# Decode keys of a paged attention turned by VectorE in 32x32 blocks inside SBUF, and scores as nine products of 32 rows

## The chip, the cores and the metric

The kernel runs on one core of a Trainium2 chip. The metric is the device time of one execution in microseconds (us); lower is better. The engines are TensorE (PE, its weight loads PEld), VectorE (DVE), ScalarE (ACT), GpSimd (POOL) and SyncE (SP). The last two also issue the transfers from the cache; SPq is SyncE's queue.

## What is computed

The reference is one decoder layer for a prompt of 1024 tokens and 8 decode sequences of 8 new tokens each: an RWKV-7 mixer, a latent attention (MLA), a pooling group, then a gated feed-forward net. The change touches the decode half of the attention. There, each of 8 sequences has 4096 old positions in pages of 128 rows (256 latent columns and 32 rope columns), found through a page table:

```python
ckv_past = cache_kv_latent[l][page_table].reshape(Bs, past_len, KV_RANK)
kr_past = cache_k_rope[l][page_table].reshape(Bs, past_len, B_ROPE_DIM)
q_lat = jnp.einsum('bthd,chd->bthc', q_nope, p['w_uk'])
s_past = (jnp.einsum('bqhc,blc->bhql', q_lat, ckv_past) + jnp.einsum('bqhr,blr->bhql', q_rope, kr_past)) * scale
s_new = (jnp.einsum('bqhc,bkc->bhqk', q_lat, ckv) + jnp.einsum('bqhr,bkr->bhqk', q_rope, kr)) * scale
s_new = jnp.where(pos[None, :] <= pos[:, None], s_new, -jnp.inf)
pr = jax.nn.softmax(jnp.concatenate([s_past, s_new], axis=-1), axis=-1)
o_lat = jnp.einsum('bhql,blc->bqhc', pr[..., :L], ckv_past) + jnp.einsum('bhqk,bkc->bqhc', pr[..., L:], ckv)
```

## The kernel before

The kernel is a sequence of stages with a barrier between them (`new_stage`, line 154). Everything here is float32. Three stages matter, and each engine's work is a list written out by hand, in order, with semaphores between the engines.

*Latent stage* (lines 641 to 834). It norms and rotates the latent rows, writes them out, and keeps three copies of the 64 new ones: by rows (`ckv_new`, line 767), latent turned (`ckvT_new`, 761) and rope turned (`krT_new`, 725 and 739).

*Queries stage* (1183 to 1255). TensorE turns `w_uk` (1212), VectorE copies it (1240), TensorE makes the latent queries of six heads (1218), and VectorE and ScalarE spread them into `q_lat` (1232). `q_rope` holds four versions of the rope queries, each on its own 32 rows with zeros elsewhere (1227).

*Decode stage* (1258 to 1571). Eight sequences are four pairs x; the two of a pair (f = 0, 1) take the two halves of 64 output rows, 6 heads x 8 tokens in each. The 32 pages of a sequence are 8 groups of four, so a pair has 8 key steps and a ninth with the new keys: 36 steps s, 32 of them with a load j. A load is, for each of the two sequences, four pages of 128 KB into a slot (128 partitions x 4 rows x 256) and their rope rows. There are five pairs of slots (NL), and loads 0 and 1 (EARLY) are issued a stage earlier. SyncE issues the transfers of f = 0 and one rope page of f = 1 (`load_rows`, 872, 875 and, the ninth, 879), GpSimd the other seven of f = 1. Each reads its page number from SBUF first. Both wait for a free slot, that is for the values of the load five before (`all_loads`, 1289).

A key step does this:

- `turn_keys` (1306): TensorE turns a slot's keys by transposes of 128x128 into three PSUM banks, eight latent (1319) and one rope (1320), once for each f. VectorE copies half (1431) and ScalarE the rest (1530, 1531) into SBUF. They wait for the copies of the half before.
- `dscores` (1322): rope products (1335), then latent products (1339), 128 rows deep, two column halves side by side, into one of two banks.
- `softmax_max` (1440): VectorE's maximum (1448) and bias (1450). Then ScalarE's exps (1539).
- `turn_weights` (1351): TensorE turns the 128x512 weights (1357), VectorE copies them (1438).
- `dvalues` (1362): weights times the rows of the slot (1375), two halves of it on either side of the turned weights; VectorE copies the part (1458).
- The nine parts of a pair are joined on VectorE (1487) while the next pair runs, then turned (1389).

TensorE's order in step s is: scores(s), keys of the next step f = 0, first half of values(s-1), keys f = 1, turned weights(s), second half of values(s-1):

```python
dscores(s)
if following:
    turn_keys(following[0] * NG + following[1], 0)
if s >= 1:
    dvalues(s - 1, 0)
if following:
    turn_keys(following[0] * NG + following[1], 1)
turn_weights(s)
if s >= 1:
    dvalues(s - 1, 1)
```

## Time and profile before

| | us |
|---|---|
| median of 3 runs | 2031.93 (2031.01 to 2033.15) |
| the profiled execution | 2032.99 |
| its span | 2031.3 |
| TensorE busy, share | 1872.9, 92% |
| VectorE busy | 979.4, 48% |
| ScalarE busy | 514.9, 25% |
| GpSimd busy | 255.5, 13% |
| queries stage | about 458 to 465 |
| decode stage | about 465 to 732 |

A line of a timeline gives the start, the duration, the engine, the line of the kernel, the operation, what it writes and reads, the tile (rows * columns of the array), the moving shape, and how many instructions are merged in it; in brackets the engine's idle time before and what ended it. A float32 product on TensorE stands as two records, each of two passes over its columns; a transpose stands as one. Ends of TensorE's records are modelled and include a tail of 0.2 to 0.3 us, in which the next ones already run. PEclk is the granted clock: 1.00 is 2.4 GHz, 0.50 is 1.2 GHz.

### The profile page before, as it was taken

Reading aid. Unit: us, or ns where it says so; the run is one execution under the profiler, and the core shown is the slowest. Engines: PE = TensorE matmul, PEld = TensorE weight load, DVE = VectorE, ACT = ScalarE, POOL = GpSimd, SP = SyncE. Lnnn points to the kernel's source line nnn. Section 1 sums busy time; section 2 is a strip of 40 time slices with the busy share of each in tenths; the row PEclk is TensorE's granted clock in tenths of the full one; section 3 lists DMA queues with packets and bytes.
Section 4 is the critical chain, followed back from the end, with each engine's and each line's share of the span. In section 5 each row is a group of like instructions: output and inputs, shape, how many; then the busy total and the mean of one; then the engine's idle time right before and its main releaser. Section 6 shows DMA issues by size and latency. Waiting matters only on the chain. (4 is left out here: it accounts for less than half of the span.)

```text
span 2031.3 us, 39649 instructions
## 1 busy us (share of the span) xinstructions
PE 1872.9 (92%) x16034; PEld 1642.3 (81%) x16034; DVE 979.4 (48%) x1800; ACT 514.9 (25%) x1064; POOL 255.5 (13%) x440
## 2 busy tenths in 40 slices
PE   5999998998999965999898979999999999999997
PEld 5999984665666632888746979999999999999996
DVE  6232426674455557544245335545545535445455
ACT  5111123542223333222124321111111111111113
POOL 1000004324444312000001210000000000000000
PEclk8999999998999965999867989999999999999999
DMA  7111113104555400000032111021021021110203
GB/s 231 53 42 53 40 43 83 33 8 129 155 156 155 119 25 0 4 4 4 18 120 64 32 32 42 22 73 37 27 63 42 27 67 32 42 53 24 64 20 110
DMA packets 148258, 119.19 MB, mean 59 GB/s; under 512 B 22900, under 2 KB 136298, under 8 KB 147805
## 3 DMA queue, kind: packets, MB, share of 16 engines
q1 hardware_dynamic: 138189, 97.35, 16.3%
q0 software_dynamic: 9744, 18.78, 3.4%
q8 instruction: 128, 2.10, 0.4%
q10 hardware_dynamic: 144, 0.52, 0.1%
q14 instruction: 53, 0.43, 0.1%
HBM read 102.81 MB, written 11.44 MB: 56 GB/s over the span
## 5 line engine op out<-in xcount | busy, mean ns | idle before, releaser
L202 PE MATMUL bank<-normed2T_hi,w_hi 128*128 128x384 f32 (+1 forms) x1056 | 346.0, 328 | 4.3 <-DVE w_lo L492 4.3
L203 PE MATMUL bank<-normed2T_hi,w_lo 128*128 128x384 f32 (+1 forms) x1056 | 345.7, 327 | 0.0
L204 PE MATMUL bank<-normed2T_lo,w_hi 128*128 128x384 f32 (+1 forms) x1056 | 345.7, 327 | 0.0
L202 PEld LDWEIGHTS bank<-normed2T_hi,w_hi 128*128 128x128 f32 x1056 | 199.1, 189 | 5.5 <-DVE w_lo L492 5.5
L203 PEld LDWEIGHTS bank<-normed2T_hi,w_lo 128*128 128x128 f32 x1056 | 199.1, 189 | 0.0
L204 PEld LDWEIGHTS bank<-normed2T_lo,w_hi 128*128 128x128 f32 x1056 | 199.0, 188 | 0.0
L202 PE MATMUL bank<-inner_hi,w_hi 128*128 128x384 f32 (+1 forms) x528 | 174.5, 330 | 10.2 <-DVE w_lo L492 7.1
L492 DVE TENSOR_TENSOR w_lo<-work,w_hi 128x1024 fp32r<-128x1024 f32 (+2 forms) x120 | 118.6, 989 | 131.1 <-ACT w_hi L487 129.9
L204 PE MATMUL bank<-inner_lo,w_hi 128*128 128x384 f32 (+1 forms) x528 | 174.0, 330 | 0.0
L203 PE MATMUL bank<-inner_hi,w_lo 128*128 128x384 f32 (+1 forms) x528 | 173.7, 329 | 0.0
L202 PE MATMUL bank<-normedT_hi,w_hi 128*128 128x384 f32 (+3 forms) x480 | 157.6, 328 | 5.6 <-DVE w_lo L492 5.6
L203 PE MATMUL bank<-normedT_hi,w_lo 128*128 128x384 f32 (+3 forms) x480 | 157.3, 328 | 0.0
L204 PE MATMUL bank<-normedT_lo,w_hi 128*128 128x384 f32 (+3 forms) x480 | 157.3, 328 | 0.0
L487 ACT CAST w_hi<-work 128x1024 fp32r<-128x1024 f32 (+2 forms) x120 | 102.3, 858 | 214.6 <-PE bank L204 209.0
L2742 DVE TENSOR_TENSOR residualT<-bank,residualT 128x384 f32<-128x384 f32 x144 | 76.1, 534 | 128.0 <-PE bank L204 127.8
L202 PEld LDWEIGHTS bank<-inner_hi,w_hi 128*128 128x128 f32 x528 | 99.6, 189 | 11.7 <-DVE w_lo L492 8.4
L2687 DVE TENSOR_TENSOR work<-bank,rwkv_streamsT 128x384 f32<-128x384 f32 (+1 forms) x66 | 33.9, 514 | 154.4 <-PE bank L204 152.2
L2658 ACT ACTIVATE rwkv_streamsT<-rwkv_streamsT 128x1088 f32<-128x1088 f32 x22 | 24.5, 1114 | 313.7 <-DVE rwkv_streamsT L2708 313.7
L203 PEld LDWEIGHTS bank<-inner_hi,w_lo 128*128 128x128 f32 x528 | 99.7, 189 | 0.0
L204 PEld LDWEIGHTS bank<-inner_lo,w_hi 128*128 128x128 f32 x528 | 99.6, 189 | 0.0
L2648 POOL COPY rwkv_streamsT<-work 128x2 f32<-128x2 f32 x22 | 4.1, 186 | 727.9 <-DVE work L2691 727.9
L202 PEld LDWEIGHTS bank<-normedT_hi,w_hi 128*128 128x128 f32 (+1 forms) x480 | 90.0, 188 | 5.9 <-DVE w_lo L492 5.7
(411 smaller groups left out, 3353.0 us busy)
## 6 DMA issues: line engine op xcount, KB each, us to landing
work<-in_w_up_dram SPq DMA_DIRECT2D x44, 512.0 KB, 3.9
residualT<-in_cache_kv_latent_dram SPq DMA_DIRECT2D x80, 128.0 KB, 2.4
residualT<-in_cache_kv_latent_dram POOLq DMA_DIRECT2D x80, 128.0 KB, 2.6
work<-in_w_in_dram SPq DMA_DIRECT2D x19, 512.0 KB, 3.8
work<-in_w_down_dram SPq DMA_DIRECT2D x32, 256.0 KB, 2.8
weight_ring<-in_cache_kv_latent_dram POOLq DMA_DIRECT2D x48, 128.0 KB, 2.6
weight_ring<-in_cache_kv_latent_dram SPq DMA_DIRECT2D x48, 128.0 KB, 2.4
residualT<-residual_spill SPq DMA_DIRECT2D x1, 4352.0 KB, 15.4
```

Source lines behind the costliest of these rows:

```text
L202: pe.matmul(out, w[0], x[0], start=first, stop=False)
L203: pe.matmul(out, w[1], x[0], start=False, stop=False)
L204: return pe.matmul(out, w[0], x[1], start=False, stop=last)
L487: act.copy(wsp[i % 2][0][:, 0:m[0], 0:m[1]], raw[:, 0:m[0], 0:m[1]]).then_inc(done, 1)
L492: dve.tensor_tensor(wsp[i % 2][1][:, 0:m[0], 0:m[1]], raw[:, 0:m[0], 0:m[1]], wsp[i % 2][0][:, 0:m[0], 0:m[1]].bitcast(F32), ALU.subtract) ...
L2648: nc.gpsimd.tensor_copy(gend[:, 0:2, f], p_seq[:, SEQ - 2:SEQ])
L2658: nc.scalar.activation(hraw, cv, ACT.Tanh, scale=0.5).then_inc(f_tanh, 1)
L2687: ins = dve.tensor_tensor(p_seq[:, t0:t0 + k], PS[g % 8][:, 0:k], rstd[:, t0:t0 + k], ALU.mult)
L2742: dve.tensor_tensor(xT[:, m, t0:t0 + n], PS[(3 * j + c) % 8][:, 0:n], xT[:, m, t0:t0 + n], ALU.add).then_inc(f_dn, 1)
```

## The change

The keys are no longer turned by TensorE. VectorE transposes each slot in blocks of 32x32 (`dve.transpose`), SBUF to SBUF, into `key_t`. In a block the columns (latent or rope) then lie on 32 partitions, and the four groups of 32 partitions hold different keys. So a score is a sum of nine products of 32 rows (eight latent, one rope), made for each of four row groups q (into PSUM banks 0 to 3) and two column halves f: 72 products of 128 columns a step. Two steps take turns in the columns of the same banks. The queries are laid out to match (`q_blk`: each block of 32 on all four groups); for that the `w_uk` blocks are spread four times ahead of the product. VectorE turns two loads before the first step, and load j + 2 after the maximum of step j. The copies of the turned weights and of the parts move from VectorE to ScalarE. The values are one piece now, ahead of the turned weights, and TensorE's order is scores(s), values(s-1), turned weights(s). The new keys are turned by VectorE in the queries stage from 288 columns. The joined result has its own place (`o_t`). The loads, their order and their waits are as before. The core of the diff:

```diff
-        PS = [ctx.enter_context(nc.psum_tensor(f"bank{i}", [P, 512], F32)) for i in range(8)]
+        banks8 = ctx.enter_context(nc.psum_tensor("bank", [P, 8 * 512], F32))
+        PS = [banks8[:, 512 * i:512 * (i + 1)] for i in range(8)]
...
+        KB = RANK // 32 + 1
+        cw = Carve(WORK - KB * QN)
+        q_blk = cw.take(KB * QN).rearrange("p (b x f c) -> p b x f c", b=KB, x=NX, f=2)
+        w_uk_b = wring[:, 0:3 * 4 * RANK].rearrange("p (m b q c) -> p m b q c", m=3, b=KB - 1, q=4)
+        o_t = spare[:, 0:2 * QN].rearrange("p (k q) -> p k q", k=2)
...
+            def rope_queries(eng_copy, groups):
+                for h in range(H):
+                    r0 = ROPE * (h % 4)
+                    for g in groups:
+                        dst = q_blk[ROPE * g:ROPE * (g + 1), KB - 1, :, :, h * TS:(h + 1) * TS]
+                        eng_copy(dst.rearrange("p x f c -> p f x c"), of_sample(rp[r0:r0 + ROPE, h // 4, SEQ:T]))
+            def latent_queries(eng_copy, h):
+                src = PS[h].rearrange("p (b f x t) -> p b f x t", b=KB - 1, f=2, x=NX)
+                for f in range(2):
+                    eng_copy(q_blk[:, 0:KB - 1, :, f, h * TS:(h + 1) * TS], src[:, :, f])
+            def spread_w(eng_copy, m):
+                src = PS[7 - m][:, 0:RANK].rearrange("p (b c) -> p b c", b=KB - 1)
+                return eng_copy(w_uk_b[:, m], src.unsqueeze(2).broadcast_to([P, KB - 1, 4, 32]))
             @block.gpsimd
             def _(pool):
-                nc.gpsimd.memset(q_rope[:, 2:4], 0.0).then_inc(s_q0, 1)
-                nc.gpsimd.memset(q_lat, 0.0).then_inc(s_q0, 1)
+                nc.gpsimd.memset(q_blk[:, :, :, :, H * TS:HD], 0.0).then_inc(s_q0, 1)
+                pool.wait_ge(s_q0, 1)
+                rope_queries(nc.gpsimd.tensor_copy, (2, 3))
...
-                for h in range(H):
-                    eng_copy(by_half(q_lat[:, k], h),
-                             of_sample(PS[4 + k + 2 * (h % 2)][:, (h // 2) * NS:(h // 2 + 1) * NS]))
+                        pe.transpose(PS[7 - m][:, k * P:(k + 1) * P],
+                                     w_uk[:, k, m * P:(m + 1) * P], ident).then_inc(wu_t, 1)
+                for m in range(3):
+                    pe.wait_ge(wu_cp, m + 1)
+                    for b in range(KB - 1):
+                        for f in range(2):
+                            r = slice(HD * f, HD * f + HD)
+                            last = pe.matmul(PS[2 * m + f][:, b * NS:(b + 1) * NS],
+                                             w_uk_b[r, m, b].rearrange("p q c -> p (q c)"), qn[r, m, SEQ:T],
+                                             start=True, stop=True)
+                    last.then_inc(ql_mm, 1)
...
-                dve.memset(q_rope[:, 0:2], 0.0).then_inc(s_qr, 1)
-                dve.wait_ge(wu_t, 1)
                 for m in range(3):
-                    dve.tensor_copy(w_ukT[:, m], PS[m][:, 0:RANK]).then_inc(wu_cp, 1)
-                dve.wait_ge(s_qr, 1)
-                rope_queries(dve.tensor_copy, (0, 1))
-                dve.wait_ge(ql_mm, 1)
-                dve.wait_ge(s_q0, 2)
-                latent_queries(dve.tensor_copy, 0)
+                    dve.wait_ge(wu_t, 2 * m + 2)
+                    spread_w(dve.tensor_copy, m).then_inc(wu_cp, 1)
+                dve.transpose(new_t, ckv_new).then_inc(s_nt, 1)
+                for m in range(3):
+                    dve.wait_ge(ql_mm, m + 1)
+                    latent_queries(dve.tensor_copy, 2 * m)
             @block.scalar
             def _(act):
-                act.wait_ge(s_q0, 1)
-                rope_queries(nc.scalar.copy, (2, 3))
-                act.wait_ge(ql_mm, 1)
-                act.wait_ge(s_q0, 2)
-                latent_queries(nc.scalar.copy, 1)
+                rope_queries(nc.scalar.copy, (0, 1))
+                for m in range(3):
+                    act.wait_ge(ql_mm, m + 1)
+                    latent_queries(nc.scalar.copy, 2 * m + 1)
...
-        keyT = cw.take(2 * 2 * 2 * 512).rearrange("p (s f k c) -> p s f k c", s=2, f=2, k=2)
-        krT = cw.take(2 * 2 * P).rearrange("p (s f c) -> p s f c", s=2, f=2)
-        pr = cw.take(2 * 512).rearrange("p (s c) -> p s c", s=2)
-        prT = cw.take(2 * 4 * P).rearrange("p (s c) -> p s c", s=2)
+        KT = 4 * RANK + P
+        key_t = cw.take(2 * 2 * KT).rearrange("p (s f c) -> p s f c", s=2, f=2)
+        pr = spare[:, 2 * QN:2 * QN + 2 * 512].rearrange("p (s c) -> p s c", s=2)
+        prT = spare[:, 2 * QN + 2 * 512:2 * QN + 4 * 512].rearrange("p (s c) -> p s c", s=2)
...
-                def turn_keys(j, f):
-                    slot = 2 * (j % NL) + f
-                    pe.wait_ge(s_k[f][j % NL], (128, 112)[f] * (j // NL + 1))
-                    if f == 1:
-                        pe.wait_ge(s_kx[j % NL], 16 * (j // NL + 1))
-                    n = 2 * j + f
-                    if n >= 1:
-                        pe.wait_ge(k_cpa, n)
-                        pe.wait_ge(k_cpb, 2 * n)
-                    rows = kslot[slot].rearrange("p (r c) -> p r c", r=4)
-                    for k in range(2):
-                        for r in range(4):
-                            pe.transpose(PS[k][:, r * P:(r + 1) * P], rows[:, r, k * P:(k + 1) * P], ident)
-                    pe.transpose(PS[2][:, 0:P], krr[:, slot, :], ident).then_inc(k_t, 1)
                 def dscores(s):
                     x, g = steps[s]
-                    bank = PS[3 + s % 2]
                     if s >= 2:
                         pe.wait_ge(dp_exp, s - 1)
-                    q = [(slice(HD * f, HD * f + HD), slice(x * P + HD * f, x * P + HD * f + HD)) for f in range(2)]
                     if g < NG:
                         j = x * NG + g
-                        pe.wait_ge(k_cpa, 2 * j + 2)
-                        pe.wait_ge(k_cpb, 4 * j + 4)
-                        for r in range(4):
-                            for f, (out, cols) in enumerate(q):
-                                pe.matmul(bank[out, r * P:(r + 1) * P], q_rope[:, r, cols], krT[:, j % 2, f, :],
-                                          start=(r == 0), stop=False, skip_group_check=True)
-                        for k in range(2):
-                            for f, (out, cols) in enumerate(q):
-                                last = pe.matmul(bank[out, :], q_lat[:, k, cols], keyT[:, j % 2, f, k, :],
-                                                 start=False, stop=(k == 1), skip_group_check=True)
-                    else:
-                        for k in range(2):
-                            for out, cols in q:
-                                pe.matmul(bank[out, 0:NS], q_lat[:, k, cols], ckvT_new[:, k], start=(k == 0),
-                                          stop=False, skip_group_check=True)
-                        for out, cols in q:
-                            last = pe.matmul(bank[out, 0:NS], q_rope[:, 2, cols], krT_new, start=False, stop=True,
-                                             skip_group_check=True)
+                        pe.wait_ge(k_t, 2 * j + 2)
+                    for b in range(KB):
+                        for q in range(4 if g < NG else 2):
+                            rows = slice(32 * q, 32 * q + 32)
+                            for f in range(2):
+                                out = PS[q][HD * f:HD * f + HD, P * (s % 2):P * (s % 2) + P]
+                                if g < NG and b < KB - 1:
+                                    keys = key_t[rows, j % 2, f, 0:4 * RANK].rearrange("p (r c) -> p r c", r=4)
+                                    keys = keys[:, :, 32 * b:32 * b + 32]
+                                    out = out.rearrange("p (r c) -> p r c", r=4)
+                                elif g < NG:
+                                    keys = key_t[rows, j % 2, f, 4 * RANK:KT]
+                                else:
+                                    keys, out = new_t[rows, 32 * b:32 * b + 32], out[:, 0:32]
+                                last = pe.matmul(out, q_blk[rows, b, x, f, :], keys, start=(b == 0),
+                                                 stop=(b == KB - 1), skip_group_check=True)
                     last.then_inc(ds_mm, 1)
...
-                def dvalues(s, part_of):
+                def dvalues(s):
...
-                pe.wait_ge(s_nm, 16)
-                turn_keys(0, 0)
-                turn_keys(0, 1)
...
-                    following = s + 1 < NSTEP and steps[s + 1][1] < NG and steps[s + 1]
                     dscores(s)
                     if g == JOINED and x >= 1:
                         turn_joined(x - 1)
-                        pe.wait_ge(j_cp, x)
-                    if following:
-                        turn_keys(following[0] * NG + following[1], 0)
                     if s >= 1:
-                        dvalues(s - 1, 0)
-                    if following:
-                        turn_keys(following[0] * NG + following[1], 1)
+                        dvalues(s - 1)
                     turn_weights(s)
-                    if s >= 1:
-                        dvalues(s - 1, 1)
-                for half in range(2):
-                    dvalues(NSTEP - 1, half)
+                dvalues(NSTEP - 1)
...
             def _(dve):
-                def copy_keys(j, f):
-                    dve.wait_ge(k_t, 2 * j + f + 1)
+                def turn_keys(j):
                     if j >= 2:
                         dve.wait_ge(ds_mm, step_of(j - 2) + 1)
-                    dve.tensor_copy(keyT[:, j % 2, f, 0, :], PS[0][:, :]).then_inc(k_cpa, 1)
-                def copy_weights(s):
-                    dve.wait_ge(dp_t, s + 1)
-                    if s >= 2:
-                        dve.wait_ge(do_mm, s - 1)
-                    n, w = (P, 4 * P) if steps[s][1] < NG else (NS, P)
-                    dve.tensor_copy(prT[0:n, s % 2, 0:w], PS[5][0:n, 0:w]).then_inc(dp_cp, 1)
+                    for f in range(2):
+                        slot = 2 * (j % NL) + f
+                        dve.wait_ge(s_k[f][j % NL], (128, 112)[f] * (j // NL + 1))
+                        if f == 1:
+                            dve.wait_ge(s_kx[j % NL], 16 * (j // NL + 1))
+                        dve.transpose(key_t[:, j % 2, f, 0:4 * RANK], kslot[slot])
+                        dve.transpose(key_t[:, j % 2, f, 4 * RANK:KT], krr[:, slot, :]).then_inc(k_t, 1)
...
-                        dve.tensor_tensor(bank[:, 0:NS], bank[:, 0:NS], newmask[:, x], ALU.add).then_inc(ds_mask, 1)
+                        dve.tensor_tensor(src, src, newmask[:, x].rearrange("p (q c) -> p q c", q=2), ALU.add
+                                          ).then_inc(ds_mask, 1)
                         dve.wait_ge(ds_mask, x + 1)
-                    dve.tensor_reduce(mx[:, x, g:g + 1], bank[:, 0:w], AX_X, ALU.max).then_inc(ds_max, 1)
+                    dve.tensor_reduce(mx[:, x, g:g + 1], src, AX_XY, ALU.max).then_inc(ds_max, 1)
...
-                copy_keys(0, 0)
-                copy_keys(0, 1)
+                dve.wait_ge(s_nm, 16)
+                turn_keys(0)
+                turn_keys(1)
                 for s in range(NSTEP):
                     x, g = steps[s]
-                    following = s + 1 < NSTEP and steps[s + 1][1] < NG and steps[s + 1]
                     softmax_max(s)
-                    for half in range(2):
-                        if following:
-                            copy_keys(following[0] * NG + following[1], half)
-                    copy_weights(s)
-                    if s >= 1:
-                        copy_part(s - 1)
+                    if g < NG and x * NG + g + 2 < len(loads):
+                        turn_keys(x * NG + g + 2)
...
+                    if g < NG:
+                        dst = pr[:, s % 2, :].rearrange("p (r q c) -> p q r c", r=4, q=4)
+                        src = banks8[:, 0:4 * 512].rearrange("p (q w) -> p q w", q=4)
+                        src = src[:, :, P * (s % 2):P * (s % 2) + P].rearrange("p q (r c) -> p q r c", r=4)
+                    else:
+                        dst, src = pr[:, s % 2, 0:NS].rearrange("p (q c) -> p q c", q=2), scores_of(s)
+                    nc.scalar.activation(dst, src, ACT.Exp, bias=bias[:, x, g:g + 1], scale=SCALE,
                                          accum_out=sums[:, x, g:g + 1]).then_inc(dp_exp, 1)
+                def copy_weights(s):
+                    act.wait_ge(dp_t, s + 1)
+                    if s >= 2:
+                        act.wait_ge(do_mm, s - 1)
+                    n, w = (P, 4 * P) if steps[s][1] < NG else (NS, P)
+                    nc.scalar.copy(prT[0:n, s % 2, 0:w], PS[4][0:n, 0:w]).then_inc(dp_cp, 1)
+                def copy_part(s):
+                    x, g = steps[s]
+                    act.wait_ge(do_mm, s + 1)
+                    if g == 0 and x >= 2:
+                        act.wait_ge(j_ready, x - 1)
+                    nc.scalar.copy(part[:, x % 2, g, :], PS[6 + s % 2][:, 0:RANK]).then_inc(do_cp, 1)
...
-                    following = s + 1 < NSTEP and steps[s + 1][1] < NG and steps[s + 1]
+                    exps(s)
                     if g == JOINED and x >= 1:
                         copy_joined(x - 1)
-                    if following:
-                        copy_keys(following[0] * NG + following[1], 0)
-                    exps(s)
-                    if following:
-                        copy_keys(following[0] * NG + following[1], 1)
+                    if s >= 1:
+                        copy_part(s - 1)
+                    copy_weights(s)
                     if g == 1 and x >= 1:
                         join_weights(x - 1)
+                copy_part(NSTEP - 1)
```

## Rows read from the trace of the kernel before

**Rows 1.** Busy time by stretch: start:end, length, PE, PEld, DVE, ACT, POOL, PEclk, DMA share, GB/s.
```profile
476.50:719.00 242.50, 235.21 (x1999) 152.68 (x1997) 120.46 (x252) 72.07 (x203) 97.90 (x198) 1.00 0.49 141
744.00:760.00 16.00, 12.49 (x29) 6.47 (x28) 9.30 (x8) 8.94 (x11) 4.89 (x2) 0.50 0.00 0
```

**Rows 2.** Timeline of TensorE over one key step.
```profile
567.79 1.09 PE L1319 MATMUL bank<-constants,weight_ring 128*128 128x128 f32 x8
...
568.92 1.08 PE L1375 MATMUL bank<-residualT,work 128*64 128x256 f32 x8
...
571.08 0.60 PE L1357 MATMUL bank<-constants,work 128*128 128x128 f32 x4
...
572.52 1.04 PE L1335 MATMUL bank<-work 128*64 128x128 f32 x16
573.39 1.89 PE L1339 MATMUL bank<-work 128*64 128x512 f32 x8
575.21 0.33 PE L1319 MATMUL bank<-constants,weight_ring 128*128 128x128 f32 x1
```

**Rows 3.** Timeline of SyncE's queue in the decode stage: load 2, its ninth, the last.
```profile
466.02 0.33 SPq L872 DMA_DIRECT2D residualT<-in_cache_kv_latent_dram  x1
...
473.15 0.32 SPq L879 DMA_DIRECT2D residualT<-in_cache_k_rope_dram  x1
474.24 0.32 SPq L872 DMA_DIRECT2D weight_ring<-in_cache_kv_latent_dram  x1
...
701.27 0.32 SPq L879 DMA_DIRECT2D residualT<-in_cache_k_rope_dram  x1
```

**Rows 4.** Transfers of the decode stage: KB each, median us to landing.
```profile
residualT<-in_cache_k_rope_dram SPq DMA_DIRECT2D x150, 16.0 KB, 2.3
```

**Rows 5.** Timeline of GpSimd: first and last large transfer of load 4.
```profile
478.87 0.49 POOL L872 DMA_DIRECT2D weight_ring<-in_cache_kv_latent_dram  x1 [0.65 <-issue]
...
484.01 0.49 POOL L872 DMA_DIRECT2D weight_ring<-in_cache_kv_latent_dram  x1 [0.64 <-issue]
```

**Rows 6.** Timelines of VectorE and ScalarE in the same step.
```profile
567.91 0.69 DVE L1448 TENSOR_REDUCE work<-bank 128x1 f32<-128x512 f32 x1 [1.25 <-PE bank L1339]
568.63 0.15 DVE L1450 TENSOR_SCALAR work<-work 128x1 f32<-128x1 f32 x1
...
573.08 0.99 DVE L1487 SCALAR_TENSOR_TENSOR work<-work 128x256 f32<-128x256 f32 x2
...
569.67 0.70 ACT L1539 ACTIVATE work<-bank,work 128x512 f32<-128x512 f32 x1
570.25 0.21 ACT L1539 ACTIVATION_READ_ACCUMULATOR work<-bank,work 128x1 f32 x1
```

**Rows 7.** Timelines of TensorE with small tiles, outside the decode stage.
```profile
811.14 0.94 PE L1892 MATMUL bank<-work,rwkv_streamsT 64*64 64x128 f32 x24
811.91 0.52 PE L1901 MATMUL bank<-rwkv_streamsT,work 64*64 64x64 f32 x24
...
748.75 1.65 PE L1685 MATMUL bank<-weight_ring 32*128 32x384 f32 x4
```

**Rows 8.** Groups of VectorE's instructions: busy us, mean ns, idle before.
```profile
L2719 DVE TENSOR_TENSOR rwkv_streamsT<-rwkv_streamsT 128x1088 f32<-128x1088 f32 x22 | 28.4, 1292 | 0.8
L1713 DVE TENSOR_TENSOR_SCAN work<-work 128x1152 f32<-128x1152 f32 x3 | 7.7, 2557 | 7.8 <-ACT work L1632 7.8
```

**Rows 9.** Timelines of TensorE and VectorE in the queries stage.
```profile
458.18 0.85 PE L1212 MATMUL bank<-constants,residualT 128*128 128x128 f32 x6 [1.55 <-PEq L158]
460.32 2.88 PE L1218 MATMUL bank<-work,weight_ring 64*128 64x64 f32 x24 [1.30 <-DVE weight_ring L1240]
...
463.24 0.88 DVE L1232 COPY work<-bank 128x64 f32<-128x64 f32 x6 [0.71 <-PE bank L1218]
```

**Rows 10.** The stage's end: VectorE's mask of step 35, the next stage's first transfer.
```profile
718.38 0.23 DVE L1446 TENSOR_TENSOR bank<-bank,residualT 128x64 f32<-128x64 f32 x1
...
732.81 0.37 SPq L1607 DMA_DIRECT2D weight_ring<-in_c_heads_dram  x1
```

101 lines of the change are left out of this document (29 added, 72 removed).

## Prediction, made before the changed kernel was seen

> **What bounds the kernel now.** I read four views in this order: the stretches of the decode stage, the timeline of TensorE over one step, the timeline of SyncE's queue, and that of GpSimd's. The stretches say that TensorE is busy 235.2 of 242.5 us at the full clock (1.00, 2.4 GHz), while VectorE is busy half of it [rows 1]. So the stage looks bound by TensorE. Its step takes 575.21 - 567.79 = 7.42 us (a quiet one 7.33): two turns of keys (each 8 + 1 transposes, about 1.1 us), two halves of the values (1.08 us each), the turned weights (0.60), the rope part of the scores (1.04) and the latent part (1.89) [rows 2].
>
> The third view changes that. SyncE issues nine transfers for each of the loads 2 to 31. After the ninth of a load (L879) the first of the next follows 1.09 to 1.10 us later in 28 of 29 cases (1.59 in the other, behind a slow issue); [rows 3] show the first of them. That is the time SyncE takes to read a page number and issue, so the wait for a free slot never holds it: SyncE is saturated from its first issue at 466.02 to its last at 701.27. The ninths are (701.27 - 473.15) / 29 = 7.87 us apart on average, 7.39 at best. **SyncE's pace is a bound of 7.87 us a load, level with TensorE's 7.33**; TensorE starts with two loads in hand and reaches the last load some 5 us after it has landed. GpSimd needs 484.01 - 478.87 = 5.14 us for a load's first to last large transfer and about 1.15 to the next load, 6.3 in all [rows 5], so it has 1.6 us of slack. The change touches no transfer. Whatever it takes off TensorE, the stage can't end before the last load has landed, 701.27 + 2.3 = 703.6 [rows 3, 4], plus the chain behind it.
>
> **The change, part by part.** *Removed per key step on TensorE:* 18 transposes (about 2.1 us) and the old scores (1.04 + 1.89, together 2.7 without overlap) [rows 2], and four copies of keys on VectorE and ScalarE (VectorE's at about 0.69 us, what its maximum over as many elements out of PSUM takes [rows 6]).
>
> *Added on TensorE:* 9 blocks x 4 row groups x 2 column halves = 72 products of 128 columns. A float32 product stands as two records, so 144. One record of 512 columns takes 1.89 / 8 = 0.24 us with two halves side by side, that is 0.43 alone (2 x 512 / 2.4 GHz); one of 128 columns then takes 0.107 alone. How many run side by side? 24 records of 128 columns on four tiles of 64x64 took 0.94 us with a tail of 0.27, so 29 ns each or a little less, near 107 / 4 [rows 7]. L1685 works on groups of 32 rows: two products of 384 columns took 1.65 us at 1.2 GHz, where one record is 0.64, so four in a row would be 2.6: neighbouring 32-row groups do overlap. Eight tiles give 144 x 107 / 8 = 1.92 us, plus tail 2.2; if only four overlap, 144 x 26.7 = 3.84, plus tail 4.1. I take 2.2, since nothing in the rows shows a limit at four.
>
> A rule that speaks against the change was weighed here. 24 records of 64 columns took 0.52 us with a tail of 0.22, 13 ns each [rows 7]. The Trainium skill (TensorEngine Tiling (Array Packing), Instruction Overhead) says that each matmul costs some 60 cycles however short it is, 25 ns at 2.4 GHz; by it the 144 records would be an estimated 3.6 us and the sum 2 to 3 us longer at its end. The row disagrees, and I go by the row.
>
> *Added on VectorE:* per load two turns of 128x1024 and two of 128x128, straight from the slots. No row shows this instruction. Two-input work in SBUF takes 1292 ns for 1088 elements, 1.19 ns each; a scan takes 2557 for 1152, 2.2 each [rows 8]. So 1.22 + 0.29 = 1.5 us a half and 3.0 a load, or at the scan's rate 2.7 and 5.4; I take the first, as moving is nearer to a plain pass than to a recurrence. A lower end (a fast plain mode) would be half. With the maximum (0.69 + 0.15) and joins (0.99) a step costs VectorE 4 to 5 us [rows 6], 7.2 at the scan's rate: under 7.87 either way. The weights' and parts' copies move to ScalarE, which has exps (0.70 + 0.21) and little else now: 0.9 + 0.7 + 0.5 = 2 us.
>
> *The new chain of a step.* From the end of scores(s): maximum and bias 0.95, exps 0.9, with two hops 2.05; meanwhile values(s-1) take 1.7 to 1.8; weights turned 0.5; scores(s+1) 2.2. Together 4.8 us, again below 7.87. VectorE now turns load j+2 between the maxima of steps j and j+1 and so waits in line for the transfer; maximum j+1 is queued behind it, and TensorE, which needs exps for its next turned weights, waits too. **The stage becomes bound by SyncE's issues alone**, with TensorE busy about 4.6 us of 7.87.
>
> *The end of the stage.* The last ninth lands at 703.6; its half is turned by 705.2; maximum 30 by 706.2; exps 707.1; weights turned 707.8; scores(31) 710.0; step 35, the last with new keys, has its scores at 710.0 + 2.05 + 0.5 + 1.2 = 713.8. Before, that point was 718.38 and the next stage's first transfer came 14.4 us later, at 732.81 [rows 10]. Behind it the new order puts one ScalarE copy ahead of the join's weights and takes one copy off VectorE: 14.9. So 728.7, **-4.1 us**, at the full clock. With TensorE idle three microseconds in every eight the clock may fall: 16 us with TensorE busy 78% ran at 0.50 [rows 1]. At 1.2 GHz scores, values and turned weights cost 4.1, 3.6 and 0.9 us and the chain is 8.4 to 9, so TensorE would fall behind, be dense, and get its clock back. The end is then 734 to 736, +1 to +3. I take the middle: -1.
>
> *The stage of the queries, ahead of it.* All of SyncE's issues wait behind it, so each microsecond here is a microsecond at the end. Before: 458.2 to 464.1 [rows 9]. After: three spread copies that write 1024 elements each (1.13 us apart, from 458.8, the first done at 460.0, the last at 462.3), the new rows' turn 0.45, then 3 x 16 products of 64 rows by 128 columns, 96 records of 64 columns where 24 took 2.88 us (0.11 each beyond the tail, clock falling to 0.5). There four records in a row used the same row group; now the group changes every two. As two groups overlap in [rows 7], 57 ns a record, 1.8 us for each of three parts: 461.9, 463.7, 465.5, then two VectorE copies, 466.7. That is +2.6. If they don't overlap: 3.5 us each, done at 471.5, +7.4. If the clock stays up, the spread copies bind: +1.3. Rope copies (12 on ScalarE, 12 on GpSimd at about 0.24) end by 463 and hide below this; uncovered they'd cost nothing, as the products end later. The latent stage loses a small GpSimd memset and copy and a VectorE copy that lay in waits, and its last copy grows by 32 columns: 0.
>
> **Sum.** -1 + 2.6 = +1.6 us on a span of 2031.3. The profiled execution took 2032.99, 1.06 above the median 2031.93, so I forecast 2034.6 for it and **2033.5 for the median**.
>
> **The rivals.** (a) *Slower by the queries' stage* (chance 0.22): products of alternate row groups don't overlap, +7.4, and TensorE's low clock at the end, +2: about 2041. For it: 0.11 us a record in [rows 9]. Against: L1685 and L1892. It decides once the stage lasts over 5 us more than before.
> (b) *Slower since TensorE's row groups or VectorE's turns bind* (0.08): with only two tiles side by side, scores take 144 x 53 ns = 7.7, the step 10.3, and 32 x (10.3 - 7.4) = +93: 2125. The same sign comes from GpSimd being held up while VectorE turns keys: 6.3 + 3.0 = 9.3 a load, +46. Against: GpSimd's 1.6 us of slack must be used up first. The Trainium skill (SBUF — State Buffer, Who interferes with whom) says that only the port pair shared by VectorE and GpSimd contends, as an exclusive lock; no row here shows whether a turn takes it.
> (c) *Faster* (0.20): SyncE's slow issues (0.47 us a load above its best of 7.39) become rarer with less going on beside them, and the clock stays up: up to -13.6, say 2023. For it: they come singly and at no fixed place. Against: the same transfers still run.
> (d) *Nothing to be seen* (0.50): my forecast, within 4 us either way. That the change does what it says is not in doubt from its text; it only doesn't touch the bound.
>
> **Range.** From 2023 (fast issues in part, full clock, +1.3) to 2044 (a queries' stage +7.4, low clock +3, turns at the scan's rate +2). Left out: (b) and half of (c). Counting 0.2% (4 us) as what a measurement can tell from no change: faster 0.20, same 0.50, slower 0.30.
>
> **What would show it.** L879's records: still 7.9 us apart, L872 following by 1.10. No wait of SyncE. TensorE busy 60 to 80% in the stage, with gaps of 2 to 3 us before the turned weights. VectorE idle until transfers land. Scores of about 2.2 us at clock 1.00; turns of about 1.2 us. The decode stage starting near 467.4. Wrong would be: L879 further apart than 8.3 (GpSimd or a slot holds it), scores over 4 us, turns over 2.4, or the queries' stage over 9 us.

## The result and the profile after

The changed kernel takes 2047.25 us at the median of 4 runs (2044.93 to 2054.67), the kernel before 2031.47 beside it (2029.04 to 2033.15): ratio 1.0081, interval 1.0066 to 1.0097. It is slower by 16 us, where 1.6 were forecast; the range ended at 2044. A second series of both gave 2047.84 and 2030.74, ratio 1.0090 (1.0075 to 1.0104). The profiled execution has a span of 2053.0 us, 21.7 more than before, and is the longest of the first four runs.

First the queue that bounds the stage. This is the timeline of SyncE's queue in the changed kernel (start, duration, engine, line): the stage's first transfer, load 2, the last ninth transfer (L873, before L879), and the first transfer of the stage behind.

```profile
472.56 0.42 SPq L1301 DMA_DIRECT2D residualT<-in_w_uv_dram  x1
473.78 0.33 SPq L866 DMA_DIRECT2D residualT<-in_cache_kv_latent_dram  x1
...
719.71 0.59 SPq L873 DMA_DIRECT2D residualT<-in_cache_k_rope_dram  x1
749.58 0.37 SPq L1572 DMA_DIRECT2D weight_ring<-in_c_heads_dram  x1
```

Beside [rows 3] and [rows 10] these four lines hold the loss. Load 2 starts at 473.78 where it started at 466.02: +7.8. Of this 0.7 lies ahead of the queries' stage, whose first transpose on TensorE starts at 458.84 where it started at 458.18 [rows 9], so the stage itself takes 7.1 us more. From load 2 to the last ninth it takes 245.9 us where it took 235.3: +10.7. From the last ninth to the next stage it takes 29.9 us where it took 31.5: -1.7. Together +16.8 at the stage's border. The rest of the kernel took 1303.4 us in this execution and 1298.5 before, +4.9; in the second profile of the changed kernel it took 1297.6, so nothing lasting stands behind that. That second profile, of a faster execution (span 2041.7), has the same three marks of SyncE's queue at

```profile
469.39 0.33 SPq L866 DMA_DIRECT2D residualT<-in_cache_kv_latent_dram  x1
716.24 0.32 SPq L873 DMA_DIRECT2D residualT<-in_cache_k_rope_dram  x1
744.15 0.37 SPq L1572 DMA_DIRECT2D weight_ring<-in_c_heads_dram  x1
```

that is +3.4, +11.6 and -3.6 beside the kernel before. The middle term is the one that stays.

The stretches of the changed kernel (columns as in [rows 1]): the products of the queries' stage, the decode stage, and its end.

```profile
460.50:471.00 10.50, 10.43 (x96) 10.32 (x96) 4.16 (x8) 2.59 (x10) 2.28 (x10) 0.50 0.01 2
479.00:720.00 241.00, 175.72 (x5118) 128.39 (x5113) 118.13 (x226) 53.92 (x138) 100.75 (x204) 0.88 0.53 147
744.00:760.00 16.00, 6.35 (x44) 2.64 (x44) 4.96 (x13) 8.11 (x9) 0.00 (x0) 0.50 0.25 77
```

TensorE is relieved: 175.7 busy us of 241, 73%, where it had 235.2 of 242.5. But its records rose from 1999 to 5118. The timelines of TensorE and of VectorE over one step of the changed kernel:

```profile
567.19 3.18 PE L1357 MATMUL bank<-residualT,mixedT 128*64 128x256 f32 x16
570.30 0.66 PE L1340 MATMUL bank<-constants,mixedT 128*128 128x128 f32 x4
570.89 2.32 PE L1330 MATMUL bank<-work 32*64 32x128 f32 x144
...
571.46 1.25 DVE L1406 STREAM_TRANSPOSE work<-weight_ring 128x1024 f32<-128x1024 f32 x1 [2.80 <-DMA residualT<-in_cache_k_rope_dram]
572.63 0.27 DVE L1407 STREAM_TRANSPOSE work<-residualT 128x128 f32<-128x128 f32 x1
```

The scores take 2.32 us, a turn 1.25 and 0.27. And VectorE's waits in the stage, longest first (total us, times, longest), name what the stage waits for: the ninth transfer of a load.

```profile
DVE work L1406 <- DMA residualT<-in_cache_k_rope_dram: 101.7, 35, 6.1
DVE work L1417 <- PE bank L1330: 12.6, 7, 3.1
```

So the stage did become bound by the arrival of the loads. What failed is the forecast that they would keep their pace. The ninths are (719.71 - 480.97) / 29 = 8.23 us apart, not 7.87, and still the next load's first transfer follows at 1.08 to 1.10 us in 28 of 29 cases: SyncE isn't waiting, it is issuing more slowly. Of the stage's 270 issues, 50 last over 0.36 us where 27 did, and the time beyond 0.32 us adds up to 21.6 us where it was 10.7. That difference, 10.9, accounts for the +10.7 of the stretch. The second profile agrees: again 8.23 us from ninth to ninth, 46 slow issues with 22.1 us.

What goes with them is in the view of the DMA queues, one queue's line (packets, MB, share), first of the kernel before over 464 to 703 us, then of the changed one over 472 to 722 us:

```profile
q8 instruction: 16, 0.26, 0.5%
```

```profile
q8 instruction: 41, 0.67, 1.2%
```

q8 fetches instructions, in packets of 16 KB. The slow issues lie at a fixed place behind them: 38 of the 41 fetches after, and 13 of the 16 before, have a slow issue that ends 1.2 to 1.9 us behind the fetch's start, with a median of 1.4 and 1.5. Fetches at random times would have met some 6 and 1. The slow issues that lie so hold 19.3 us of excess after and 7.7 before; all the others hold 2.3 after and 3.0 before. So the whole increase belongs to issues behind a fetch, and each fetch costs about the same in either kernel, 0.47 and 0.48 us. One of them, in the changed kernel (queue q8 over 566.5 to 567.0 us, and SyncE's queue):

```profile
q8 instruction: 1, 0.02, 14.6%
```

```profile
566.38 0.32 SPq L866 DMA_DIRECT2D weight_ring<-in_cache_kv_latent_dram  x1
566.89 1.23 SPq L869 DMA_DIRECT2D residualT<-in_cache_k_rope_dram  x1
```

The number of fetches fits the code. TensorE has 2 x 5118 instructions in the stretch, a weight load with each record; 41 packets make 250 for each. Before it was 2 x 1999 and 16, again 250. The Trainium skill (Runtime: NRT & Kernel Launch, Instruction fetch mechanics) says that fetches come in blocks of 16 KiB, 256 instructions; the rows agree. It also says that they are hidden behind the pace of the instructions. Whether that holds for the engine that fetches was not looked at; here another engine's queue shows them, 10.9 us / 25 = 0.44 us for each more.

### The profile page after: what moved, and what is told of

It reads as the page before. It is cut to its first block and busy times, and to the rows that moved or that the text cites. A ratio compares the mean times of both kernels' runs of the same rounds, so it can differ in the third digit from the quotient of the medians.

```text
span 2053.0 us, 46577 instructions
## 1 busy us (share of the span) xinstructions
PE 1825.5 (89%) x19610; PEld 1631.7 (79%) x19610; DVE 987.2 (48%) x1779; ACT 500.8 (24%) x1008; POOL 257.0 (13%) x449
## 5 line engine op out<-in xcount | busy, mean ns | idle before, releaser
L1330 PE MATMUL bank<-work 32*64 32x128 f32 x4608 | 92.0, 306 | 20.3 <-issue 15.8
L1330 PEld LDWEIGHTS bank<-work 32*64 32x64 f32 x4608 | 80.6, 148 | 29.8 <-issue 24.7
```

Of the source, the lines that this page charges most:

```text
L1330: last = pe.matmul(out, q_blk[rows, b, x, f, :], keys, start=(b == 0), stop=(b == KB - 1), skip_group_check=True)
```

## Experiments

The experiments set one theory against its rivals. **Theory I:** SyncE's issuing bounds the changed kernel's stage; with it goes theory F, that it was slowed by the fetches for TensorE's larger number of instructions. **The rivals:** something behind it binds as well (TensorE at a low clock, VectorE, GpSimd), or the slowing comes from VectorE's turns. The queries' stage was a question of its own.

### Does SyncE's issuing bound? One of nine issues moved, in either kernel

The ninth transfer goes to ScalarE, behind its copy of the parts:

```diff
-            if f == 0:
+            if f == 0 and ninth:
...
-                    load_rows(eng, j, f)
+                    load_rows(eng, j, f, ninth=False)
...
                     if s >= 1:
                         copy_part(s - 1)
+                        x0, g0 = steps[s - 1]
+                        if g0 < NG and x0 * NG + g0 + NL < len(loads):
+                            ninth(x0 * NG + g0 + NL)
```

> The changed kernel with the ninth transfer of each load (the rope rows of group 1's fourth page) issued by ScalarE after its copy of the parts, not by SyncE: SyncE issues 8 transfers a load instead of 9, nothing else moves. In the changed kernel the distance from one ninth to the next is 8.23 us on average over 29, and SyncE goes from the ninth to the next load's first in 1.10 us in 28 of 29, so it never waits. Theory I (SyncE's issuing bounds the stage): one of nine issues and its page load gone, the pace drops to 7.1 to 7.4 us a load, the stage is 24 to 33 us shorter and the kernel 2015 to 2024 us. Rival V (TensorE, VectorE or the DMA queues of GpSimd bind just behind): pace 7.8 to 8.2, kernel within 12 us of the changed one.

Measured: 2018.16 us (2011.21 to 2023.16), 0.9949 of the kernel before (0.9926 to 0.9972), 29 us below the changed kernel (27 by the two ratios). From load 2's first issue to load 31's the pace is (675.80 - 465.65) / 29 = 7.25 us a load, 8.23 in the changed kernel. This is theory I, inside both its ranges: one issue in nine, with its page load, is worth 1.0 us a load. The whole +0.36 a load of the change is smaller than that.

> The same move made in the kernel before: the ninth transfer issued by ScalarE at the end of a key step. Before, SyncE's pace is 7.87 us a load, and TensorE is busy 235.2 of 242.5 us of the stage, so its own need is 7.35 us a load or less. Theory I: SyncE no longer binds, TensorE does, at 7.35 to 7.6 us a load; kernel 6 to 14 us faster than before. Rival T (TensorE already is the bound there, and SyncE's pace follows it): 0 to 2 us. Both say that the move gains more in the changed kernel than here, by 12 us or more under I.

Measured: 2030.71 us, 1.0006 of the kernel before (0.9995 to 1.0017). Rival T was right here: theory I's 6 to 14 us did not come. The stretch of the decode stage, and SyncE's waits in it:

```profile
476.50:719.00 242.50, 234.96 (x1993) 152.20 (x1991) 119.66 (x249) 72.06 (x203) 98.00 (x199) 1.00 0.49 140
```

```profile
SPq L864 <- PE bank L1375: 29.4, 18, 5.6
```

Now SyncE waits 29.4 us for free slots, which come free by TensorE's values (L1375), and TensorE is busy 235 of 242.5 us exactly as in [rows 1]. So before the change TensorE bound the stage, and SyncE, which never waited either, ran at nearly the same pace beside it. A queue that never waits is not by that the only bound; taking an issue from it told the two apart.

### What slows SyncE's issues? Fewer and more instructions on TensorE, no turns on VectorE

Fewer: the scores of the key steps are summed over 5 of the 9 blocks; the first four are left out.

```diff
-                    for b in range(KB):
+                    for b in (range(4, KB) if g < NG else range(KB)):
...
```

> The changed kernel with only 5 of the 9 blocks of 32 rows in the scores of the key steps (the first four blocks of the latent rows left out of the sum). One look, for SyncE's pace in the decode stage. Theory F (what slowed SyncE from 7.87 to 8.23 us a load are TensorE's instructions: the stage's instruction fetches rose from 16 to 41 with TensorE's records from 1999 to 5118, and SyncE's issues longer than 0.36 us from 27 to 50, their excess over 0.32 us from 10.7 to 21.6 us, 0.44 us for each more fetch): 2048 records fewer, 25 fetches, excess 14 to 15 us, pace 7.99 us a load. Rival D (VectorE's turns of 32x32, or the clock, slow SyncE): the excess stays 20 us or more and the pace 8.15 or more.

Measured: 2036.67 us (a single run), pace (709.23 - 479.44) / 29 = 7.92 us a load, 30 slow issues, 12.1 us of excess. The queue of instructions over 472 to 712 us:

```profile
q8 instruction: 26, 0.43, 0.8%
```

That is theory F's 25 fetches, with the same turns on VectorE and the same transfers; the slowing shrank somewhat more than expected (7.99 and 14 to 15 were forecast).

No turns: the latent rows are turned for the first two loads only; the later scores use those old keys.

```diff
-                        dve.transpose(key_t[:, j % 2, f, 0:4 * RANK], kslot[slot])
+                        if j < 2:
+                            dve.transpose(key_t[:, j % 2, f, 0:4 * RANK], kslot[slot])
```

> The changed kernel with the turns of the latent rows by VectorE left out after the first two loads (scores are then of old keys; the rope rows are still turned). One look. Theory F: SyncE's excess and pace stay as they are, 20 us or more and 8.15 to 8.3 us a load, though VectorE is 78 us less busy. Rival D (VectorE's turns hold up SyncE or the transfers): excess near 11 us, pace near 7.87.

Measured: 2047.9 us (a single run), pace 8.13, 45 slow issues with 18.1 us of excess. The stretch of the stage, and the queue of instructions over 474 to 720 us:

```profile
481.00:717.00 236.00, 174.49 (x5103) 126.51 (x5108) 54.65 (x166) 53.92 (x138) 99.87 (x202) 0.88 0.52 149
```

```profile
q8 instruction: 42, 0.69, 1.1%
```

VectorE is busy 54.7 us in place of 118 and the pace hardly moves; the excess is 3 us less, below what F allowed (20) and far from D's 11. The excess scatters by as much without any such edit: in the five profiles that issue nine transfers a load on SyncE with the turns and the products of the scores in place it is 18.7 to 23.0 us, at paces of 8.16 to 8.30. VectorE's turns are not the cause. Nor is the clock: it is 0.88 here as in the changed kernel, and 0.86 with five blocks, where the loads came faster.

More: each product of the key steps' scores in two halves. The instructions are all there, but their sums are no longer the scores (why was not settled), so it is read for its time alone.

```diff
...
+                                    for c in range(2):
+                                        last = pe.matmul(out[:, :, w * c:w * c + w], q_blk[rows, b, x, f, :],
+                                                         keys[:, :, w * c:w * c + w], start=(b == 0),
+                                                         stop=(b == KB - 1), skip_group_check=True)
```

> The changed kernel with each product of the key steps' scores cut in two halves of 64 columns (144 products a step in place of 72, same work). One look. Theory F: 4608 records more in the stage, 77 fetches, SyncE's excess 37 us, pace 8.77 us a load, the stage some 15 us longer. Rival D: excess and pace as in the changed kernel, 21.6 us and 8.17 to 8.26. TensorE itself has room: its scores take 2.3 to 3.5 us of 8.2 a load, twice that would be 7.0 at the most beside 2.9 for the rest, so at the low clock it could bind; then SyncE's gap between loads would rise over 1.10 us.

Measured: 2135.25 us (a single run), where theory F expected some 15 us over the changed kernel. The stretch, the longest wait of VectorE, and the queue of instructions over 472 to 787 us:

```profile
480.00:785.00 305.00, 249.58 (x8927) 190.90 (x8925) 113.32 (x219) 52.44 (x131) 99.95 (x202) 0.80 0.40 117
```

```profile
DVE work L1426 <- PE bank L1335: 187.8, 29, 8.0
```

```profile
q8 instruction: 72, 1.18, 1.6%
```

VectorE waits 188 us for the scores, none of its long waits is for a transfer any more, and SyncE waits for slots (gaps of up to 8.4 us): TensorE binds, at (784.23 - 479.48) / 29 = 10.5 us a load. The fetches came (72 for 77), SyncE's excess rose to 29.8 us (37 expected), but with a queue that waits a slow issue costs nothing, so the pace tests neither theory. One thing it does show: halving the streamed columns did not halve a product's price. The next section finds the same of other products.

| kernel | fetches in the stage | slow issues, excess us | of it behind a fetch | us a load |
|---|---|---|---|---|
| before | 16 | 27, 10.7 | 7.7 | 7.87 |
| five blocks | 26 | 30, 12.1 | 9.9 | 7.92 |
| changed | 41 | 50, 21.6 | 19.3 | 8.23 |
| no turns | 42 | 45, 18.1 | 16.9 | 8.13 |
| two halves | 72 | 51, 29.8 | 29.5 | 10.5 (TensorE) |

The column "of it behind a fetch" counts the excess of slow issues that end 1.2 to 1.9 us behind a fetch's start. It is 0.38 to 0.48 us for each fetch in all five kernels; the differences between neighbouring rows are no finer than the scatter just named.

These runs change the number of TensorE's instructions and its fetches together; that it is the fetches, and not TensorE's activity, rests on where the slow issues lie. Why a fetch holds up an issue on another engine was not settled.

### What do the products of the queries' stage cost?

The products of 64 rows by 128 columns cut in two halves of 64 weight columns (the first kernel), or in two halves of 32 streamed columns with all 128 weight columns loaded for each (the second). The diff is the first kernel's:

```diff
-                            last = pe.matmul(PS[2 * m + f][:, b * NS:(b + 1) * NS],
-                                             w_uk_b[r, m, b].rearrange("p q c -> p (q c)"), qn[r, m, SEQ:T],
+                            for c in range(2):
+                                last = pe.matmul(PS[2 * m + f][64 * c:64 * c + 64, b * NS:(b + 1) * NS],
+                                                 w_uk_b[r, m, b, 2 * c:2 * c + 2].rearrange("p q c -> p (q c)"),
+                                                 qn[r, m, SEQ:T], start=True, stop=True)
```

> The changed kernel with the products of the queries' stage cut in two halves of 64 weight columns each (192 records of 64*64 in place of 96 of 64*128; same work). In the changed kernel the 96 records take 10.51 us, 107 to 109 ns each, at a granted clock of 0.50 throughout. Theory W (a record costs its 128 weight columns, one after another, and 64*64 tiles go beside each other as the 24 records of 64*64 of the output projection do in 0.52 and 0.94 us, 22 to 39 ns each): 192 records take 4.2 to 7.5 us, the decode stage's first transfer comes 3 to 6 us earlier, the kernel is 3 to 6 us faster than the changed one. Rival S (products of 64 rows don't go beside each other in any tiling; a record costs its columns in full, 53 ns at half the size): 192 records take 10.2 us or more, no gain.

> The changed kernel with each product of the queries' stage cut in two halves of 32 streamed columns instead, with the same 128 weight columns loaded for each (192 records). One look, for the stage's products alone. If the loading of 128 weight columns sets the 107 ns, the 192 records take 20.5 us (107 ns each). If loading and streaming add up (64 and 64 columns' worth), 15 to 16 us. If only streaming counts (the two row groups not overlapping), 10.5 us or less (53 ns each).

> The changed kernel itself, on the same chip as the next run, to see what the earlier 5.4 us of the decode stage's start are worth in the kernel's time. 1.0075 to 1.0085 of the kernel before, 2046 to 2049 us.

> The changed kernel with the queries' products in 64*64 tiles again. Its profiled run showed the 192 products in 4.7 us, the decode stage's first transfer at 468.41 in place of 473.78 us and the next stage's first at 744.12 in place of 749.58, but its median was only 1.6 us below the changed kernel's, with runs 12 us apart. If the 5.4 us hold to the end, 4.5 to 6 us faster than the changed kernel beside it. If the low granted clock comes later or elsewhere and takes them back: 0 to 3 us.

The timeline of TensorE in that stage, of the changed kernel in its first and in its second profile, of the weight halves (second series), and of the streamed halves (2050.09 us, a single run):

```profile
460.57 10.51 PE L1231 MATMUL bank<-work,weight_ring 64*128 64x64 f32 x96 [0.88 <-DVE weight_ring L1212]
```

```profile
461.11 5.58 PE L1231 MATMUL bank<-work,weight_ring 64*128 64x64 f32 x96 [0.88 <-DVE weight_ring L1212]
```

```profile
459.19 2.82 PE L1232 MATMUL bank<-work,weight_ring 64*64 64x64 f32 x146 [0.88 <-DVE weight_ring L1212]
462.50 0.92 PE L1232 MATMUL bank<-work,weight_ring 64*64 64x64 f32 x46 [0.49 <-issue]
```

```profile
459.19 18.23 PE L1232 MATMUL bank<-work,weight_ring 64*128 64x32 f32 x192 [0.88 <-DVE weight_ring L1212]
```

The clock over these products in the first profile stands in the stretch shown above (0.50); in the second it is 1.00:

```profile
461.10:466.70 5.60, 5.58 (x96) 5.44 (x96) 3.99 (x7) 2.53 (x10) 2.22 (x10) 1.00 0.01 3
```

And over 463 to 467 us of the kernel with the streamed halves:

```profile
463.00:467.00 4.00, 4.00 (x41) 4.00 (x40) 0.76 (x2) 0.65 (x2) 0.00 (x0) 0.50 0.00 0
```

Three things follow. The same 96 records cost 109 ns each at 1.2 GHz and 58 ns at 2.4 GHz. Halving the streamed columns with the weight columns kept leaves a record at 98 ns at 1.2 GHz (4.00 us for 41), where 107 was expected of the loading alone, 80 if loading and streaming added up, and 53 of the streaming alone. So **the price is, nearly all of it, the loading of 128 weight columns, one record after another**, though they lie in 64 rows and take turns between two row groups. The Trainium skill (TensorE: Matmul & The Clock Gate, LDWEIGHTS (loading the stationary operand)) gives the time as columns divided by 1.2, independent of the rows, 107 ns; the row at 1.2 GHz agrees, the one at 2.4 GHz shows half of it. And in 64*64 tiles a record costs 19 ns, 146 in 2.82 us: tiles of this size do go beside each other, theory W.

What this is worth is read from the stage's own length, from its first transpose on TensorE to load 2, since the stage doesn't start at the same time in every execution (455.6 to 459.4 over the twelve profiles of the changed kernel and its variants). The first transposes of the changed kernel in its two profiles and of the weight halves in the second series:

```profile
458.84 0.84 PE L1224 MATMUL bank<-constants,residualT 128*128 128x128 f32 x6 [1.56 <-PEq L159]
459.38 0.85 PE L1224 MATMUL bank<-constants,residualT 128*128 128x128 f32 x6 [1.55 <-PEq L159]
457.46 0.85 PE L1224 MATMUL bank<-constants,residualT 128*128 128x128 f32 x6 [1.55 <-PEq L159]
```

Load 2 follows at 473.78, 469.39 and 466.14. So the stage takes 14.9 us at the low clock and 10.0 at the full one, where the kernel before took 7.8 (466.02 - 458.18), and 8.7 with the weight halves (9.2 in their first profile, from 459.23 to 468.41). In both profiles of the halves the clock over the products was 1.00. The change costs the stage +7.1 at the low clock and +2.2 at the full one, and the halves leave +0.8 to +1.3 of it.

In the kernel's time the halves gave 2045.66 us (2040.29 to 2052.55) in the first series, 1.0085 of the kernel before (1.0055 to 1.0116) beside the changed kernel's 1.0081: no gain to be seen. In the second series they gave 2044.63 beside 2047.84, 1.0068 (1.0056 to 1.0080) beside 1.0090 (1.0075 to 1.0104): 3 to 4.5 us, with intervals that overlap a little, and less than the 4.5 to 6 expected. A gain of that size fits a stage that is 0.8 to 1.3 us shorter in executions with the full clock and 5.8 to 6.3 in those with the low one, (if the halves keep the full clock, as in their two profiles), but the kernel's time alone doesn't show it. Which executions the low clock meets wasn't settled: the six profiles with this unchanged part show 0.50 in four and 1.00 in two. In each of them the clock falls once about here, between 459.1 and 469.9 us, in four ahead of nearly all these products and in two behind them.

### Together, and how far the issues can be moved

Queries' products in 64*64 tiles and two transfers a load on ScalarE (the ninth, and the rope rows of group 0's fourth page):

```diff
-                if f == 0 or q < 3:
+                if q < 3 or f == 0 and ninth:
...
+                    page = load_page(act, 0, j, 3)
+                    act.dma_start(krr[96:P, 2 * (j % NL), :], kr_pages[bass.ds(page, 1)].rearrange("a p c -> (a p) c")
+                                  ).then_inc(s_k[0][j % NL], 16)
```

> The changed kernel with the queries' products in 64*64 tiles, the ninth transfer of each load on ScalarE, and the rope rows of group 0's fourth page on ScalarE too: SyncE issues 7 transfers a load. With the ninth alone moved the pace was 7.25 us a load and the stage's SyncE still never waited. Theory I (SyncE's issuing goes on binding): pace 6.3 to 6.5, stage 22 to 28 us shorter than with 8 issues, and 4 to 5 us from the queries' stage: kernel 1985 to 1993 us. Rival V (GpSimd's seven transfers a load, VectorE's 4 us of turns and reductions behind the wait, or TensorE at 5.4 us a load at the low clock take over): pace 6.8 or more, kernel 1998 to 2013 us, and SyncE's gap between loads over 1.10 us.

Measured: **1995.14 us** (1993.78 to 1995.88), 0.9823 of the kernel before (0.9805 to 0.9840). From load 2's first issue to load 31's the pace is (656.95 - 466.08) / 29 = 6.58 and SyncE has no wait in the stage: theory I's mechanism, with a kernel 2 us and a pace 0.1 us beyond its figures. The next two kernels ask what binds after that. Four transfers on ScalarE, between the copy of the parts and that of the weights:

> Four of the 16 transfers of a load on ScalarE (the rope rows of the third and fourth page of both groups), 6 left on SyncE and 6 on GpSimd, and the queries' products in 64*64 tiles. In the run with two on ScalarE, SyncE's pace was 6.60 us a load, and GpSimd, whose seven issues take some 6.3 to 6.8 us a load, waited for nothing either. Theory I (the two queues' issuing still binds): pace 5.7 to 6.0, the stage 17 to 26 us shorter, kernel 1969 to 1978 us. Rival A (ScalarE's four issues of 1.05 us each, between its copy of the parts and its copy of the weights, lengthen the chain of a step: TensorE and VectorE wait for them): pace 6.3 or more, kernel 1986 us or more.

Measured: 2030.52 us (2026.51 to 2038.48), ratio 1.0000 (0.9988 to 1.0013), pace (687.63 - 466.21) / 29 = 7.64: all of the gain is gone. ScalarE's timeline shows where:

```profile
563.66 0.37 ACT L1511 COPY work<-bank 128x256 f32<-128x256 f32 x1 [1.36 <-PE bank L1358]
564.33 3.82 ACTq L1530 DMA_DIRECT2D residualT<-in_cache_k_rope_dram  x4
568.25 0.59 ACT L1504 COPY mixedT<-bank 128x512 f32<-128x512 f32 x1 [4.22 <-issue]
```

The weights' copy, which TensorE's values wait for, starts 4.22 us late, behind the issues. Over the stage it stood so in 27 of 33 copies, 110.6 us in all: rival A. The last kernel puts the issues behind that copy, and balances the queues (ScalarE 3, SyncE 7 with four page loads, GpSimd 6):

```diff
                     copy_weights(s)
+                    if s >= 1:
+                        x0, g0 = steps[s - 1]
+                        if g0 < NG and x0 * NG + g0 + NL < len(loads):
+                            moved(x0 * NG + g0 + NL)
```

> Three transfers of a load on ScalarE (both of the fourth page of group 0, the rope rows of the fourth page of group 1), 7 on SyncE with four page loads in place of five (the rope rows of group 1's third page come to it), 6 on GpSimd, and ScalarE issues them behind its copy of the weights, not between the copies of the parts and of the weights, where four of them cost 4.2 us of waiting a step and brought the pace to 7.5. Queries' products in 64*64 tiles. Theory C (it was the place in the chain that cost, and the queues' issuing that bounds otherwise): SyncE 6.6 - 0.6 for the page load and fewer issues, GpSimd 5.7: pace 5.9 to 6.2 us a load, kernel 1972 to 1984 us. Rival A (ScalarE's issues lengthen the step wherever they stand, since its exponentials come right after): pace 6.6 or more, kernel 1995 us or more.

Measured: 1996.70 us (1989.59 to 2000.77), 0.9841 (0.9825 to 0.9858), pace (659.64 - 471.56) / 29 = 6.49. With the issues behind the copy, and one fewer of them, 34 us are back: much of what was lost went with their place in the chain, though place and number were changed together. But theory C's 5.9 to 6.2 us a load and 1972 to 1984 us were not reached: the time lies in rival A's range (1995 or more), the pace between the two. The reason is in the counts. The expectation took 0.6 us off SyncE for a page load and fewer issues, but the kernel with two transfers moved already had seven issues and four page loads on SyncE, since the ninth's page load went with it; this one has the same seven and four. Its best load takes SyncE 5.81 us where it took 5.86 there, its slow issues add 0.57 us a load (16.5 us in all) where they added 0.71, and it waits for a slot for 0.3 us in all. By these counts SyncE's issuing goes on setting the pace in both, and nothing was gained because nothing was taken from it. GpSimd, with six issues, has gaps of up to 3.7 us for which the profile names no cause.

## Why the prediction was wrong, step by step

- **SyncE's issuing bounds the stage: the bound was real, its size was taken as fixed.** This is the step that failed. "The change touches no transfer", so the prediction kept 7.87 us a load; it was 8.23, +10.7 us over the stage, two thirds of the loss. Without these 10.7 us the measured median would be 2036.6, inside the range. The text had the doubt in hand, 0.47 us a load of slow issues in [rows 3]'s queue, and used it only downwards, in rival (c), "with less going on beside them". It never asked what the slow issues follow. The view of the queues had a lead, 16 fetches of instructions, 13 of them just ahead of a slow issue, and the diff multiplies TensorE's instructions in the stage by 2.6. The sign that was to show the forecast wrong, ninths further apart than 8.3 us, was set too wide to catch it.
- **"Level with TensorE's 7.33"** was half right: before the change TensorE was the bound and SyncE ran level with it (moving an issue gained nothing), after it SyncE alone was (moving one gained 29 us). That the gain on TensorE would buy nothing is what happened.
- **The queries' stage: the term is near by luck at the full clock, and mis-sized at the low one.** +2.6 was taken, for row groups that overlap at the low clock, 57 ns a record; +7.4 was the bound without overlap. Measured from the stage's first transpose: +7.1 at the low clock, without overlap, 109 ns a record, and +2.2 at the full one, 58 ns a record. So the overlap that the term rests on did not come, and where +2.6 is nearly met, a clock does it that the term didn't count on. The row used ([rows 7], 64*64 tiles) has 64 weight columns, and cutting the new products to 64 weight columns made them overlap as well; uncut they have 128, as L1218's in [rows 9], which had already shown 0.11 us a record. The nearer row was set aside for the farther one. Rival (a)'s reason, two row groups not overlapping, is what happened; its sign, a stage over 5 us longer, held in the first profile, and it was given 0.22. By itself it makes no more than half of the loss.
- **The scores on TensorE:** 2.2 us forecast, 2.32 measured (144 records, 16 ns each); four side by side would have been 4.1. The rule that was weighed against it, of the Trainium skill (TensorEngine Tiling (Array Packing), Instruction Overhead), would make an estimated 3.6; the trace disagrees.
- **The turns on VectorE:** 1.22 + 0.29 forecast, 1.25 + 0.27 measured, hidden behind the wait for the transfers. No sign of GpSimd held up (rival (b)): leaving the turns out changed the pace by 0.1 us.
- **The end of the stage:** -4.1 at the full clock, +1 to +3 at the low one, -1 taken. Measured from last ninth to next stage: -1.7 in the first profile and -3.6 in the second (716.24 to 744.15).
- **The clock in the stage:** 0.88, TensorE busy 73% of it; forecast as "may fall". It didn't set the pace: with five blocks the clock was lower (0.86) and the pace better.

The sum with the measured sizes, at the stage's border, from what lies ahead of the queries' stage to the end: 0.7 + 7.1 + 10.7 - 1.7 = +16.8 us in the first profile, 1.2 + 2.2 + 11.6 - 3.6 = +11.4 in the second (744.15 beside 732.81). The first terms, 0.7 and 1.2, are where these executions stood when the stage began. The medians of the two series differ by 15.8 and 17.1; the two profiles are the slowest and the fastest execution of their series.

## What to carry to other kernels

Splitting a product into many small ones has a price outside TensorE: its instructions must be fetched, and here each 16 KB of them went with some 0.4 to 0.5 us lost on an engine that does nothing but issue transfers; so count instructions before and after, and look at the instruction queue beside the slow issues of whatever bounds. When a queue never waits, move one item off it (and count what is left on it, page loads too) before calling it the bound: in the kernel before this gained nothing, in the changed one 29 us. When an issue is moved to a busy engine, put it behind the copy that others wait for, and take a product's price from a row with the same number of weight columns, not the same number of rows.

## What the runs showed of the hardware

- Behind most fetches of instructions (16 KB, some 250 of TensorE's) an issue of SyncE is late: it ends 1.2 to 1.9 us behind the fetch's start, by 0.1 to 1.2 us later than usual (38 of 41 fetches in the changed kernel, 13 of 16 before). Over 25 more fetches that made 0.44 us each.
- Products of 64 rows by 128 weight columns and 64 streamed ones cost 109 ns a record at 1.2 GHz and 58 at 2.4, and 98 at 1.2 GHz with only 32 streamed: the weight columns set most of it. In 64*64 tiles: 19 ns at the full clock.
- TensorE stayed at 1.2 GHz (granted clock 0.50) through 10.5 us in which it was busy without a gap (stretch 460.5 to 471), and through 14.4 us in the kernel with streamed halves (463.0 to 477.4). In other executions of the same code it ran at 2.4 GHz.
- Eight tiles of 32 rows by 64 columns: 144 records of 128 streamed columns in 2.32 us, 16 ns each.
- ScalarE issues four transfers with their page loads in 4.2 us, 1.05 each; SyncE needs 1.10 for a page load and an issue.
